# Dividing attention weights by their sums ahead of the transposition, and moving selection counts from one engine to another

## The chip, the core and the metric

The kernel runs on one core of one Trainium2 chip. The metric is the device time of one execution in microseconds (us), of the slowest core where there are several; here there is one. The engines are TensorE (PE: matmuls; PEld is its weight load), VectorE (DVE), ScalarE (ACT), GpSimd (POOL) and SyncE (SP, which issues most DMA transfers). Each runs its own list of instructions in order; they wait for each other on semaphores.

## The reference: what is computed

One inference step of a hybrid decoder of two layers, in float32, for two groups of requests that share the weights: one prompt of 512 tokens, and 8 samples of 8 tokens each with 2048 tokens of past in a paged cache. The width is 1024, with 16 query heads on 2 key/value heads (groups of 8), head dimension 64. Each layer is half an FFN (width 2688), a mixer, half an FFN. Layer 0 uses mixer A, layer 1 mixer B.

Mixer A keeps, for each query, the keys with the highest indexer scores: 128 for a prompt query, 256 of the 2056 for a sample's query. Mixer B is an attention over a window of 128 tokens with one sink per head:

```python
def sink_softmax(logits, sinks):
    m = max(max(logits, axis=-1), sinks)
    e = exp(logits - m)
    return e / (sum(e, axis=-1) + exp(sinks - m))

def sparse_attend(q, k_sel, v_sel, dist, table):     # mixer A
    logits = q @ k_sel * HEAD_DIM ** -0.5 + rel_bias(dist, table)
    return softmax(where(dist >= 0, logits, NEG)) @ v_sel

def swa_prompt(...):                                 # mixer B, blocks of 128 queries
    logits = qb @ band(k) * HEAD_DIM ** -0.5 + bias  # 256 keys, the block's and the one before
    o = sink_softmax(where(valid, logits, NEG), sinks) @ band(v)
```

## The kernel before

Activations lie feature-major in SBUF (128 features by 576 tokens: 512 of the prompt, 64 of the samples), and each weight tile is split by POOL into a high and a low part, which PE multiplies in three passes (lines 593 to 597). This takes most of the time; the change doesn't touch it.

**Prompt attention.** One function per engine, used by both mixers with `L` "A" or "B". Its work is 32 units `(r, i, g)`: four blocks `i` of 128 queries, taken in `ORDER` (0 to 3 in A, 3 to 0 in B; `r` counts the blocks as they are taken), and in each eight heads `g` per key/value head `n`. A unit is one `g` for both `n`. Block `i` in mixer A has `128 * (i + 1)` keys; in mixer B 256, and 128 in block 0. A unit goes through:
- logits on PE (strip of biases by a matmul with an identity, L745; in A for `i > 0` a mask, L740; queries by keys, L749), into the PSUM buffer `PS[u % 2]`;
- the negated row maximum on DVE (L1599), in B then a minimum with the negated sink (L1602);
- exponentials on ACT with their row sums (L1215), into `p`;
- transposition of the weights on PE (L775), copy to SBUF on ACT (`weights_of`, L1249);
- values on PE (L789), which leaves the block's unscaled outputs in PSUM.

At the end of a block the row sums are inverted (L1568; in B the sinks' exponentials `es` are added first), PE spreads the inverses over the rows (`row_scales`, L758), ACT copies them to `otok` (L1224, two halves), DVE multiplies them with the outputs (`products`, L1576, halves issued in the next block's units 1 and 2) and makes the low parts (`parts`, L1589). The high parts `XH` are made by ACT in A (L1231) and by DVE in B. The order of the instructions is written out by hand in these loops: on PE `transposed(u)`, `logits(u + 2)`, `values(u - 1)`, and `row_scales` between them in a block's last unit.

**Selection for the samples.** Beside mixer A's prompt units, the threshold of the samples' 256 best keys is found bit by bit, a step each: `decide(k)` on DVE (L1833 to L1845, small operations on one column) and then `count(k + 1)`, a pass over 1032 columns of scores. Steps up to `FOUND` = 7 come before the prompt attention; then one step follows each unit's maximum (`after(u)`, `selections`). Counts 1 to `SIGN_COUNTS` = 16 are done by ACT as sums of signs (L1375, output `maskSA`), nine of them (8 to 16) in the loop of units by

```python
def later_counts(u):
    if FOUND + 1 + u <= SIGN_COUNTS:
        count(FOUND + 1 + u)
```

the later ones by DVE itself (L1826). After the last bit, `threshold`, `sample_cut`, `sample_mask` and `block_diagonal` (the samples' queries `qbd`, spread over a zeroed tile, L1549) take a unit each.

**Samples.** `paged_sample_attention` begins on PE with `new_logits()` (L842: the samples' new keys), then transposes pages of keys (L825, `keys(b, c)`); in B, `window_sample_attention` begins with its transpositions (L912).

Of the kernel before, what the change touches and what calls it, by code (L numbers as in the profile page):

```python
# [17 lines left out]
F32 = mybir.dt.float32  # L18
# [92 lines left out]
def mixer_memory(sb, L):  # L111
# [6 lines left out]
    with ExitStack() as c:  # L118
# [79 lines left out]
        else:  # L198
# [5 lines left out]
            mb(c, "stripL", [P, KVH, GRP, 2 * P], F32R)  # L204
            with ExitStack() as c2:
                mb(c2, "stripH", [P, KVH, GRP, 2 * P], F32R)
# [4 lines left out]
            mb(c, "striproom", [P, KVH * GRP * 2 * P])  # L211
            mb(c, "vT", [P, TOK])
            with ExitStack() as c2:
                mb(c2, "strip", [P, KVH, GRP, 2 * P])
            mb(c, "p", [P, 2, KVH, SEQ])
            mb(c, "pt", [P, 2, KVH, 2, P])
            mb(c, "otok", [P, GRP, P])
# [5 lines left out]
def bass_hybrid_step(nc, io):  # L223
    at = layout()
    ctx = ExitStack()
    with ctx:
# [37 lines left out]
        with ExitStack() as c:  # L264
# [36 lines left out]
                "pt_ps", "pt_evac", "pv_ps", "ri_set", "r_ps", "r_set", "o_evac", "ot_evac", "ktS_ps", "ktS_evac", "qkS_ps", "nmS_set",  # L301
# [3 lines left out]
                      "cm_used", "seek_set", "count_set", "oh_set", "newS_ps", "newS_set", "riS_set") + tuple(f"kv_in{s}{c}" for s in range(KV_SLOTS)  # L305
                                                                   for c in range(KT_GROUPS)),
                "B": ("es_in", "es_set", "kv_in", "ptnS_evac", "esS_in", "esS_set")}
# [220 lines left out]
        def _(pool):  # L528
# [29 lines left out]

            ffn("ffn0")
            for c in range(A_CHUNKS):  # L560
                split(at["inA"][0] + c, None, 0, ND * (IDIM + IH) if c == 0 else ND * P)
            for n in range(KVH):
# [6 lines left out]
                .then_inc(MS["A"]["selb_in"], 16)  # L569
            pool.wait_ge(MS["A"]["qk_ps"], NQT * GRP)  # L570
# [14 lines left out]
        def _(pe):  # L585
# [136 lines left out]
            def prompt_attention(L, m, ms, aend):  # L722
                units = [(r, i, g) for r, i in enumerate(ORDER[L]) for g in range(GRP)]
# [4 lines left out]
                def logits(u):  # L728
                    r, i, g = units[u]
                    k0, nk = key_range(L, i)  # L730
# [4 lines left out]
                    masked, w = L == "A" and i > 0, min(nk, 2 * P)  # L735
# [7 lines left out]
                    for n in range(KVH):  # L743
                        for k, part in enumerate((m["stripH"][:, n], strip_low(L, n))):
                            mm(PS[u % 2][:, n, nk - w:nk], m["identr"][:, :], part[:, g, 2 * P - w:2 * P],  # L745
                               start=k == 0 and not masked, stop=False)
# [16 lines left out]
                turned = turned_counts(L)  # L763

                def transposed(u):

                    r, i, g = units[u]
                    nk = key_range(L, i)[1]
                    for n in range(KVH):
                        pe.wait_ge(ms["p_set"], 2 * u + n + 1)  # L770
                        out, free = turned_place(L, u, n, nk)
# [8 lines left out]
                def values(u):  # L780

                    r, i, g = units[u]
                    k0, nk = key_range(L, i)
# [3 lines left out]
                    for k in range(nk // P):  # L787
                        for n in range(KVH):
                            ins = mm(bank[6 + g // 4][n * HD:(n + 1) * HD, g % 4 * P:(g % 4 + 1) * P],  # L789
                                     m["kvtok"][:, k0 // P + k, KVW + n * HD:KVW + (n + 1) * HD],  # L790
                                     weights_of(L, u)[:, n, k, :], start=k == 0, stop=k == nk // P - 1)
# [16 lines left out]

            def paged_sample_attention(m, ms):
                LG = sample_logits  # L810
                pe.wait_ge(ms["o_evac"], 2 * NQT)
                pe.wait_ge(ms["qbd_set"], 1)
                pe.wait_ge(ms["maskS_set"], 1)
                pe.wait_ge(ms["selb_in"], 16)
# [24 lines left out]
                def new_logits():  # L839
                    for b in range(NB):  # L840
# [65 lines left out]
            def window_sample_attention(m, ms):  # L906

                pe.wait_ge(ms["o_evac"], 2 * NQT)
# [7 lines left out]
                for k, group in enumerate(LOGIT_GROUPS):  # L916
# [6 lines left out]
                    ins.then_inc(ms["qkS_ps"], 1)  # L923
                for half in range(2):
# [145 lines left out]
            prompt_attention("A", m, ms, aend)  # L1070
# [17 lines left out]
            prompt_attention("B", m, ms, aend)  # L1088
# [14 lines left out]
        def _(act):  # L1103
# [89 lines left out]
            def attention_loads(m, ms):  # L1193

                act.wait_ge(g_out, 32)
                act.dma_start(m["strip"].rearrange("p n g x -> p (n g) x"),
# [7 lines left out]
            def prompt_attention(L, m, ms, after):  # L1204
                units = [(r, i, g) for r, i in enumerate(ORDER[L]) for g in range(GRP)]
                turned = turned_counts(L)

                def exps(u):
                    r, i, g = units[u]
                    nk = key_range(L, i)[1]  # L1210
# [16 lines left out]
                def high_parts(r):  # L1227
                    i = ORDER[L][r]
# [6 lines left out]
                for u, (r, i, g) in enumerate(units):  # L1235
                    if u + 1 < len(units):
                        exps(u + 1)
                    if L == "A" and r and g == 2:
                        high_parts(r - 1)
                    if L == "B" and g == GRP - 2:  # L1240
                        act.wait_ge(ms["es_in"], r + 1)
# [851 lines left out]
```

## Time and profile before

| | |
|---|---|
| Median of 3 runs | 2341.34 us (2338.2 to 2345.47) |
| Profiled execution: time, span | 2343.02 us, 2341.2 us |
| PE busy | 2258.6 us (96%), 14801 instructions |
| PEld busy | 2029.8 us (87%) |
| DVE busy | 1137.1 us (49%) |
| POOL busy | 1029.7 us (44%) |
| ACT busy | 415.4 us (18%) |
| Chain that ended last | PE 61%, DVE 2% |

The span is the trace's time from first to last instruction, and the time is what the device reports for the same execution. Busy shares are averages over the whole span: a stage in which PE waits shows only when the trace is read by stretches. The chain is followed back from the last instruction to what released each step; its shares by line are those of the weight matmuls (lines 593 to 597, 57% together).

### The profile page before, as it was taken

How to read it: one execution, taken by the hardware profiler on the slowest of the kernel's cores; microseconds unless marked ns; L12 is line 12 of the kernel's file. 1: busy time of each engine (PE TensorE's matmuls, PEld its weight loads, DVE VectorE, ACT ScalarE, POOL GpSimd, SP SyncE). 2: the span in 40 equal slices, each digit the busy share in tenths (PEclk: the TensorE clock that was granted, in tenths of full speed). 3: DMA queues.
4: the chain of work that ended last, by engine and by line, in shares of the span. 5: the costliest groups of instructions: out<-in, count | busy, mean ns of one | idle time of the engine just before them, and what ended most of it. 6: DMA issues, size and time to landing. Idle time of an engine off the chain costs nothing.

```text
span 2341.2 us, 39794 instructions
## 1 busy us (share of the span) xinstructions
PE 2258.6 (96%) x14801; PEld 2029.8 (87%) x14819; DVE 1137.1 (49%) x1811; ACT 415.4 (18%) x848; POOL 1029.7 (44%) x622
## 2 busy tenths in 40 slices
PE   7999999999888899999999999999999999999997
PEld 6999989959666588999999999999996689999997
DVE  4544522488584546555512555542264465555311
ACT  3101000131554412010000101000015420101002
POOL 4546455414001024555555555555541055555552
PEclk9999999999799999999999999999999899999998
DMA  5435363535003433333223333322350023333221
GB/s 125 99 73 115 78 155 89 114 64 147 10 1 100 130 89 77 86 81 81 78 84 90 82 86 85 81 78 82 94 154 23 1 73 81 81 86 83 79 83 60
DMA packets 378042, 196.33 MB, mean 84 GB/s; under 512 B 66531, under 2 KB 374476, under 8 KB 377932
## 3 DMA queue, kind: packets, MB, share of 16 engines
q1 hardware_dynamic: 366108, 180.79, 31.3%
q10 hardware_dynamic: 11552, 13.71, 2.0%
q8 instruction: 62, 1.02, 0.2%
q0 software_dynamic: 288, 0.56, 0.1%
q14 instruction: 32, 0.26, 0.0%
HBM read 192.23 MB, written 11.64 MB: 87 GB/s over the span
## 4 chain that ended last, share of the span: by engine, by line
PE 61%; DVE 2%; ACTq 0%; ACT 0%; issue 0%; DVEq 0%
PE psum L594 17%; PE psum L597 11%; PE psum L595 10%; PE psum L593 10%; PE psum L596 9%; PE psum L749 1%; PE psum L775 1%; DVE XS L1448 1%; PE psum L745 1%; PE psum L789 1%; ACTq L1200 0%; PE psum L758 0%; DVE squares L1481 0%; PE psum L939 0%; PE psum L938 0%
## 5 line engine op out<-in xcount | busy, mean ns | idle before, releaser
L545 POOL CAST WSP<-WST 128x1024 fp32r<-128x1024 f32 (+1 forms) x305 | 310.5, 1018 | 1250.0 <-PE psum L597 1008.8
L547 POOL TENSOR_TENSOR WSP<-WST,WSP 128x1024 fp32r<-128x1024 f32 (+1 forms) x305 | 709.3, 2326 | 24.5
L594 PE MATMUL psum<-XS,WSP 128*128 128x512 f32 x1672 | 658.4, 394 | 0.0
L593 PE MATMUL psum<-XS,WSP 128*128 128x320 f32 x1672 | 520.4, 311 | 9.5 <-DVE XS L1448 4.3
L597 PE MATMUL psum<-XS,WSP 128*128 128x320 f32 x1672 | 522.7, 313 | 0.0
L595 PE MATMUL psum<-XS,WSP 128*128 128x320 f32 x1672 | 519.2, 311 | 0.0
L596 PE MATMUL psum<-XS,WSP 128*128 128x256 f32 x1672 | 474.0, 283 | 0.0
L596 PEld LDWEIGHTS psum<-XS,WSP 128*128 128x128 f32 x1672 | 314.8, 188 | 71.5
L593 PEld LDWEIGHTS psum<-XS,WSP 128*128 128x128 f32 x1672 | 321.4, 192 | 11.6 <-DVE XS L1448 5.2
L597 PEld LDWEIGHTS psum<-XS,WSP 128*128 128x128 f32 x1672 | 321.5, 192 | 0.0
L594 PEld LDWEIGHTS psum<-XS,WSP 128*128 128x128 f32 x1672 | 314.4, 188 | 0.4
L595 PEld LDWEIGHTS psum<-XS,WSP 128*128 128x128 f32 x1672 | 314.2, 188 | 0.0
L594 PE MATMUL psum<-GS,WSP 128*128 128x512 f32 x672 | 265.3, 395 | 0.0
L1465 DVE TENSOR_TENSOR us<-psum,rstd 128x576 f32<-128x576 f32 x84 | 63.6, 758 | 396.7 <-PE psum L597 396.5
L1488 DVE SCALAR_TENSOR_TENSOR X<-psum,X 128x576 f32<-128x576 f32 x48 | 36.4, 757 | 416.1 <-PE psum L597 416.1
L1179 ACT ACTIVATE gs<-gs 128x576 f32<-128x576 f32 x84 | 57.6, 686 | 923.1 <-DVE gs L1471 923.1
L593 PE MATMUL psum<-GS,WSP 128*128 128x320 f32 x672 | 205.9, 306 | 2.9 <-POOL WSP L547 2.9
L597 PE MATMUL psum<-GS,WSP 128*128 128x320 f32 x672 | 206.7, 308 | 0.0
L595 PE MATMUL psum<-GS,WSP 128*128 128x320 f32 x672 | 205.7, 306 | 0.0
L1528 DVE TENSOR_TENSOR us<-us,gs 128x576 f32<-128x576 f32 x84 | 187.7, 2235 | 2.9
L596 PE MATMUL psum<-GS,WSP 128*128 128x256 f32 x672 | 189.1, 281 | 0.0
L596 PEld LDWEIGHTS psum<-GS,WSP 128*128 128x128 f32 x672 | 126.3, 188 | 29.8
(325 smaller groups left out, 2595.0 us busy)
## 6 DMA issues: line engine op xcount, KB each, us to landing
WST<-in_ffn_w_gate SPq DMA_DIRECT2D x168, 256.0 KB, 3.9
WST<-in_ffn_w_up SPq DMA_DIRECT2D x168, 256.0 KB, 3.9
WST<-in_ffn_w_down SPq DMA_DIRECT2D x192, 224.0 KB, 3.5
WST<-in_a_w_in SPq DMA_DIRECT2D x28, 256.0 KB, 4.4
kv0A<-in_cache_kv SPq DMA_DIRECT2D x48, 128.0 KB, 2.3
kv2A<-in_cache_kv SPq DMA_DIRECT2D x48, 128.0 KB, 2.3
WST<-in_b_w_in SPq DMA_DIRECT2D x20, 256.0 KB, 4.0
kscr<-in_cache_idx SPq DMA_DIRECT2D x128, 32.0 KB, 2.1
```

The lines of the kernel that those rows point to most:

```text
L545: nc.gpsimd.tensor_copy(WSP[s][:, 0, 0:width], WST[s][:, 0:width]).then_inc(w_hi, 1)
L547: nc.gpsimd.tensor_tensor(WSP[s][:, 1, 0:width], WST[s][:, 0:width], WSP[s][:, 0, 0:width].bitcast(F32), ALU.subtract).then_inc(w_split, 1)
L593: mm(front, high, x[:, 0, 0:FRONT], start=first, stop=False)
L594: mm(split, high, x[:, :, FRONT:TOK], start=first, stop=False)
L595: mm(front, high, x[:, 1, 0:FRONT], start=False, stop=False)
L596: mm(back, low, x[:, 0, FRONT:TOK], start=False, stop=last)
L597: return mm(front, low, x[:, 0, 0:FRONT], start=False, stop=last)
L745: mm(PS[u % 2][:, n, nk - w:nk], m["identr"][:, :], part[:, g, 2 * P - w:2 * P], start=k == 0 and not masked, stop=False)
L1179: fn(gs[:, j % 2, :], gs[:, j % 2, :], ACT.Silu).then_inc(silu_done, 1)
L1465: steps.mark(tt(dst, acc(k)[rows], r, ALU.mult))
L1488: steps.done(stt(X[:, d, :], acc(aend + d % 2), scale, X[:, d, :], ALU.mult, ALU.add))
L1528: steps.done(tt(us[:, :], us[:, :], g, ALU.mult))
```

## The change

Two parts.

**Mixer B** gets prompt functions of its own. The sink becomes a column: the strip of biases has 258 columns instead of 256 (`SINK` = 2, the second a mask), so the maximum and the row sum of the exponentials include it, and the minimum, `es` and their waits go. Each unit's weights are multiplied by the inverse of their sums on DVE (`factors`) before PE transposes them. `row_scales`, `otok` and `products` are gone; ACT copies the outputs from PSUM to `XH`, DVE makes `XL` from PSUM and `XH`. PE's order becomes logits two units ahead, values of the unit before, transposition.

**Mixer A** keeps its functions. All counts after `FOUND` are DVE's (`later_counts` is gone), a block's last unit (`g` = 7) has no step, and the inverses of a block are computed before the next block's first maximum instead of after. `block_diagonal` is done by POOL, ahead of the output projection's weights. On PE the samples begin with the key transpositions and wait for one product only; `new_logits` follows them and takes the other waits.

The pieces of the diff below are, in this order: the build on POOL; PE's order in mixer B; PE's start of the samples in mixer A; ACT's copies in B; ACT's counts in A; the place of the inverses on DVE in A; DVE's multiplications in B; the sign of the counts; and the steps that a block's last unit skips.

```diff
+            def block_diagonal(m, ms):
+
+                pool.wait_ge(acc_evac, at["inA"][1] + A_CHUNKS + RING)
+                nc.gpsimd.memset(m["qbd"][:, :, :], 0.0).then_inc(ms["qbd_clear"], 1)
+                pool.wait_ge(ms["qbd_clear"], 1)
+                for n in range(KVH):
+                    h = slice(n * HD, (n + 1) * HD)
+                    dst = m["qbd"][h].rearrange("p b (n g t) -> p n g b t", n=KVH, g=GRP)[:, n]
+                    nc.gpsimd.tensor_copy(dst, m["qT"][h, :, SEQ:TOK].rearrange("p g (b t) -> p g b t", b=NB))\
+                        .then_inc(ms["qbd_set"], 1)
...
+                logits(0)
+                logits(1)
+                for u in range(len(units)):
+                    if u + 2 < len(units):
+                        logits(u + 2)
+                    if u:
+                        values(u - 1)
+                    transposed(u)
+                values(len(units) - 1)
...
-                new_logits()
                 keys(0, 0)
                 keys(0, 1)
                 keys(0, 2)
+                new_logits()
                 logits(0, 0)
...
+                    if g == 5:
+                        high_part(r, 0)
+                    if g == 1 and r:
+                        high_part(r - 1, 1)
...
-            def later_counts(u):
-
-                if FOUND + 1 + u <= SIGN_COUNTS:
-                    count(FOUND + 1 + u)
...
+                    if g == 0 and r:
+                        row_scales(r - 1)
                     dve.wait_ge(ms["qk_ps"], u + 1)
                     ins = nc.vector.tensor_reduce(nm, PS[u % 2][:, :, 0:nk], AX, ALU.max, negate=True)
-                    if g == 0 and r:
-                        row_scales(r - 1)
...
+                def factors(u):
+
+                    r, i, g = units[u]
+                    dve.wait_ge(ms["p_set"], 2 * (u + 1))
+                    nc.vector.reciprocal(m["ri"][:, i, :, g], m["rs"][:, i, :, g]).then_inc(ms["ri_set"], 1)
+                    dve.wait_ge(ms["ri_set"], u + 1)
+                    for n in range(KVH):
+                        p = m["p"][:, u % 2, n, 0:key_range("B", i)[1]]
+                        ts(p, p, m["ri"][:, i, n, g:g + 1], None, ALU.mult).then_inc(ms["pn_set"], 1)
...
             def sign(k):
-                return -2 ** 31 if 1 <= k <= SIGN_COUNTS else 0
+                return -2 ** 31 if 1 <= k <= FOUND else 0
...
             def selections(u):
 
-                k = found + u
+                if u % GRP == GRP - 1:
+                    return
+                k = found + u - u // GRP
```

The order of the instructions shows the change at three places. First DVE in mixer A, at units 0 and 1, where a step follows each maximum (`nmA`); before:

```order
L1599 TENSOR_REDUCE nmA<-psum 128x2 [waits qk_psA,strip_inA,dve_step]
L1833 STREAM_SHUFFLE countA<-countA 128x1 [waits count_setA]
L1840 TENSOR_SCALAR seekA<-countA 128x1 [waits dve_step]
L1841 SCALAR_TENSOR_TENSOR seekA<-seekA 128x1 [waits dve_step]
L1845 TENSOR_SCALAR seekA<-seekA 128x1 [waits seek_setA]
L1599 TENSOR_REDUCE nmA<-psum 128x2 [waits qk_psA,dve_step]
```

and now:

```order
L1706 TENSOR_REDUCE nmA<-psum 128x2 [waits qk_psA,strip_inA,dve_step]
L1968 STREAM_SHUFFLE countA<-countA 128x1 [waits count_setA]
L1975 TENSOR_SCALAR seekA<-countA 128x1 [waits dve_step]
L1976 SCALAR_TENSOR_TENSOR seekA<-seekA 128x1 [waits dve_step]
L1980 TENSOR_SCALAR seekA<-seekA 128x1 [waits seek_setA]
L1961 TENSOR_SCALAR flagsA,countA<-scsA,seekA 128x1032 [waits seek_setA,dve_step]
L1706 TENSOR_REDUCE nmA<-psum 128x2 [waits qk_psA]
```

Between two maxima the count (`flagsA,countA`) has joined the decision, and the next maximum's wait for the step is gone with it.

Second PE in mixer B, where one block of queries ends and the next begins (`ptB` are the transposed weights, `riB` the inverses of the sums); before:

```order
L775 MATMUL psum<-ident,pB 128x128 [waits pt_evacB,p_setB]
L775 MATMUL psum<-ident,pB 128x128
L758 MATMUL psum<-ident,riB 64x128 [waits ri_setB]
L758 MATMUL psum<-ident,riB 64x128 x15
L789 MATMUL psum<-ptB,kvtokB 64x128 [waits pt_evacB]
L789 MATMUL psum<-ptB,kvtokB 64x128 x3
L745 MATMUL psum<-stripHB,identrB 128x256 [waits r_setB,p_setB]
L745 MATMUL psum<-stripLB,identrB 128x256
L745 MATMUL psum<-stripHB,identrB 128x256
L745 MATMUL psum<-stripLB,identrB 128x256
L749 MATMUL psum<-kTB,qTB 128x256 x2
```

and now:

```order
L837 MATMUL psum<-stripHB,identrB 128x258 [waits p_setB]
L837 MATMUL psum<-stripLB,identrB 128x258
L837 MATMUL psum<-stripHB,identrB 128x258
L837 MATMUL psum<-stripLB,identrB 128x258
L841 MATMUL psum<-kTB,qTB 128x256 x2
L871 MATMUL psum<-ptB,kvtokB 64x128 [waits ot_evacB,pt_evacB]
L871 MATMUL psum<-ptB,kvtokB 64x128 x3
L857 MATMUL psum<-ident,pB 128x128 [waits pt_evacB,pn_setB]
L857 MATMUL psum<-ident,pB 128x128
L857 MATMUL psum<-ident,pB 128x128 [waits pt_evacB,pn_setB]
```

The sixteen small matmuls of the scales are gone, the transposition waits for the multiplied weights (`pn_setB`), and it stands behind the logits and values instead of ahead of them.

Third DVE in mixer B at the same place (`esB` are the sinks' exponents); before:

```order
L1599 TENSOR_REDUCE nmB<-psum 128x2 [waits qk_psB]
L1602 TENSOR_TENSOR nmB<-nmB,nsinkB 128x2 [waits dve_step]
L1608 TENSOR_TENSOR esB<-nmB,nsinkB 128x16 [waits nm_setB]
L1599 TENSOR_REDUCE nmB<-psum 128x2 [waits qk_psB]
L1602 TENSOR_TENSOR nmB<-nmB,nsinkB 128x2 [waits dve_step]
L1567 TENSOR_TENSOR rsB<-rsB,esB 128x16 [waits es_setB,p_setB]
L1568 RECIPROCAL riB<-rsB 128x16 [waits dve_step]
L1576 TENSOR_TENSOR otokB<-psum,otokB 128x512 [waits pv_psB,r_setB]
```

and now:

```order
L1741 TENSOR_REDUCE nmB<-psum 128x2 [waits qk_psB]
L1722 RECIPROCAL riB<-rsB 128x2 [waits p_setB]
L1726 TENSOR_SCALAR pB<-pB,riB 128x256 [waits ri_setB]
L1726 TENSOR_SCALAR pB<-pB,riB 128x256
L1733 TENSOR_TENSOR XS<-psum,XS 128x4x128 [waits oh_setB]
L1741 TENSOR_REDUCE nmB<-psum 128x2 [waits qk_psB]
```

The minimum, the additions of the sinks and the products have given way to a reciprocal of two columns and two multiplications behind each maximum.

## Rows read from the trace of the kernel before

**Rows 1.** By stretches: us, busy PE, PEld, DVE, ACT, POOL (x), PEclk, DMA share, GB/s.
```profile
595.40:624.20 28.80, 23.30 (x114) 16.36 (x114) 10.16 (x53) 18.80 (x57) 0.00 (x0) 0.58 0.01 2
688.70:726.40 37.70, 33.51 (x319) 24.09 (x318) 21.30 (x29) 21.82 (x52) 6.74 (x4) 1.00 0.15 43
1763.80:1785.20 21.40, 20.88 (x184) 14.90 (x186) 10.00 (x24) 13.69 (x46) 1.97 (x1) 1.00 0.11 26
```

**Rows 2.** Waits, 595 to 730: us in total, times, longest.
```profile
DVE countA L1833 <- ACT maskSA L1375: 21.7, 9, 2.9
```

**Rows 3.** Timeline, mixer A's first block: start us, duration us, [idle before, releaser].
```profile
598.08 0.43 DVE L1599 TENSOR_REDUCE nmA<-psum 128x2 f32<-128x256 f32 x1
...
609.27 0.42 DVE L1599 TENSOR_REDUCE nmA<-psum 128x2 f32<-128x256 f32 x1
...
610.25 0.83 PE L775 MATMUL psum<-ident,pA 128*128 128x128 f32 x2 [0.60 <-ACT pA L1215]
...
610.70 1.16 ACT L1375 ACTIVATE maskSA<-scwA,seekA 128x1032 bf16<-128x1032 f32 x1
...
611.99 0.01 DVE L1833 LOAD_MASK_SELECT countA<-countA  x1 [2.29 <-ACT maskSA L1375]
```

**Rows 4.** Timeline of DVE, mixer A's second block.
```profile
646.92 0.69 DVE L1599 TENSOR_REDUCE nmA<-psum 128x2 f32<-128x512 f32 x1
...
647.53 0.15 DVE L1833 STREAM_SHUFFLE countA<-countA 128x1 f32<-128x1 f32 x1
...
648.35 1.29 DVE L1826 TENSOR_SCALAR_CACHE_REDUCE flagsA<-scsA,seekA 128x1032 bf16<-128x1032 f32 x1
```

**Rows 5.** Timeline, mixer A's first change of blocks.
```profile
623.41 0.69 DVE L1599 TENSOR_REDUCE nmA<-psum 128x2 f32<-128x512 f32 x1
...
625.32 1.16 ACT L1375 ACTIVATE maskSA<-scwA,seekA 128x1032 bf16<-128x1032 f32 x1
...
627.83 0.60 ACT L1224 ACTIVATE otokA<-psum 128x512 f32<-128x512 f32 x1 [0.78 <-PE psum L758]
...
628.53 0.38 PE L740 MATMUL psum<-pmaskA,identb 128*128 128x256 bf16 x2 [0.53 <-issue]
...
630.05 0.69 DVE L1599 TENSOR_REDUCE nmA<-psum 128x2 f32<-128x512 f32 x1 [1.94 <-PE psum L749]
...
636.10 0.68 DVE L1599 TENSOR_REDUCE nmA<-psum 128x2 f32<-128x512 f32 x1
```

**Rows 6.** Timeline of DVE, mixer A's fourth block.
```profile
705.99 0.91 DVE L1549 MEMSET qbdA<- 128x1024 f32 x1 [0.16 <-issue]
```

**Rows 7.** Timeline of PE, start of mixer A's samples.
```profile
727.26 0.18 PE L842 MATMUL psum<-maskSA,selbA 128*128 128x8 bf16 x1 [0.86 <-DVE otokA L1576]
...
729.26 2.28 PE L825 MATMUL psum<-ident,kv0A 128*128 128x128 f32 x12
```

**Rows 8.** Timeline of PE, mixer B.
```profile
1780.32 0.66 PE L775 MATMUL psum<-ident,pB 128*128 128x128 f32 x4
...
1782.01 0.66 PE L789 MATMUL psum<-ptB,kvtokB 128*64 128x128 f32 x8
...
1782.59 0.66 PE L775 MATMUL psum<-ident,pB 128*128 128x128 f32 x4
...
1787.48 0.66 PE L775 MATMUL psum<-ident,pB 128*128 128x128 f32 x4
...
1840.09 0.68 PE L775 MATMUL psum<-ident,pB 128*128 128x128 f32 x2
...
1844.50 1.09 PE L912 MATMUL psum<-ident,kvB 128*128 128x128 f32 x8 [0.99 <-DVE otokB L1576]
```

**Rows 9.** Timeline of POOL and DVE ahead of mixer A.
```profile
586.55 4.68 POOL L566 TENSOR_TENSOR WSP<-stripA,stripHA 128x2048 fp32r<-128x2048 f32 x1 [1.67 <-PE psum L597]
...
587.25 3.99 DVE L1841 SCALAR_TENSOR_TENSOR seekA<-seekA 128x1 int32<-128x1 int32 x1
```

**Rows 10.** Groups by line and form, DVE: busy us, mean ns | idle before.
```profile
L1764 DVE TENSOR_SCALAR squares<-rPA,wisA 128x384 f32<-128x384 f32 x1 | 0.4, 420 | 1.0 <-ACT rPA L1360 1.0
```

More of the change, by code:

```diff
@@ L734, in logits @@
                         pe.wait_ge(ms["r_set"], 2 * r)
-                    masked, w = L == "A" and i > 0, min(nk, 2 * P)
+                    masked, w = i > 0, min(nk, 2 * P)
                     if masked:
@@ L807, in prompt_attention, with window_prompt_attention, logits, transposed @@
                 values(len(units) - 1)
+            def window_prompt_attention(m, ms, aend):
+                units = [(r, i, g) for r, i in enumerate(ORDER["B"]) for g in range(GRP)]
+                pe.wait_ge(acc_evac, aend + RING)
+                pe.wait_ge(ms["kvt_sb"], NTT)
+                pe.wait_ge(ms["vnew_sb"], 2)
+                def logits(u):
+                    r, i, g = units[u]
+                    k0, nk = key_range("B", i)
+                    if u > 1:
+                        pe.wait_ge(ms["p_set"], 2 * (u - 1))
+                    if u == 0:
+                        pe.wait_ge(ms["strip_set"], KVH)
+                    for n in range(KVH):
+                        for k, part in enumerate((m["stripH"][:, n], strip_low("B", n))):
+                            mm(PS[u % 2][:, n, 0:nk + SINK], m["identr"][:, :], part[:, g, 2 * P - nk:STRIP_B],
+                               start=k == 0, stop=False)
+                    for n in range(KVH):
+                        h = slice(n * HD, (n + 1) * HD)
+                        ins = mm(PS[u % 2][:, n, 0:nk], m["qT"][h, g, i * P:(i + 1) * P], m["kT"][h, k0:k0 + nk],
+                                 start=False, stop=True)
+                    ins.then_inc(ms["qk_ps"], 1)
+                turned = turned_counts("B")
+                def transposed(u):
+                    r, i, g = units[u]
+                    nk = key_range("B", i)[1]
+                    for n in range(KVH):
+                        pe.wait_ge(ms["pn_set"], 2 * u + n + 1)
+                        out, free = turned_place("B", u, n, nk)
+                        if free >= 0:
+                            pe.wait_ge(ms["pt_evac"], turned[free] if nk <= 2 * P or n else turned[free] - 1)
+                        for k in range(nk // P):
+                            ins = nc.tensor.transpose(out[:, k * P:(k + 1) * P], m["p"][:, u % 2, n, k * P:(k + 1) * P],
+                                                      ident[:, :])
+                        if n or nk > 2 * P:
+                            ins.then_inc(ms["pt_ps"], 1)
+                def values(u):
+                    r, i, g = units[u]
+                    k0, nk = key_range("B", i)
+                    pe.wait_ge(ms["pt_evac"], turned[u])
+                    if g % 4 == 0 and r > 0:
+                        pe.wait_ge(ms["ot_evac"], 2 * (r - 1) + g // 4 + 1)
+                    for k in range(nk // P):
+                        for n in range(KVH):
+                            ins = mm(bank[6 + g // 4][n * HD:(n + 1) * HD, g % 4 * P:(g % 4 + 1) * P],
+                                     m["kvtok"][:, k0 // P + k, KVW + n * HD:KVW + (n + 1) * HD],
+                                     weights_of("B", u)[:, n, k, :], start=k == 0, stop=k == nk // P - 1)
+                    ins.then_inc(ms["pv_ps"], 1)
+                logits(0)
[7 more added lines that the diff above has]
+                values(len(units) - 1)
@@ L1555, in block_diagonal, with paged_prompt_attention @@
                 ins.then_inc(ms["qbd_set"], 1)
[L1557 to L1558 removed]
+            def paged_prompt_attention(m, ms, between, after):
+                units = [(r, i, g) for r, i in enumerate(ORDER["A"]) for g in range(GRP)]
                 def row_scales(r):
[L1562 removed]
+                    i = ORDER["A"][r]
                     dve.wait_ge(ms["p_set"], 2 * GRP * (r + 1))
                     rs, ri = m["rs"][:, i], m["ri"][:, i]
[L1565 to L1567 removed]
                     nc.vector.reciprocal(ri, rs).then_inc(ms["ri_set"], 1)
```

181 lines of the change are left out of this document (112 added, 69 removed).

## The prediction

> **What bounds the kernel now.** I read the busy shares and the chain of waits first: TensorE (PE) is busy 96% of the span and nearly all of the chain is its own, so a change gains only where PE stands still or is made to do less. The two prompt stages are the places to look, and the view by stretches shows them. In mixer A's first block of queries (595.4 to 624.2 us) PE is busy 23.3 of 28.8 us at 0.58 of its clock: at about half rate. In its last block it is busy 33.5 of 37.7 us at full clock; in mixer B's first block 20.9 of 21.4 us [rows 1]. The list of waits for mixer A names the idle time: VectorE (DVE) waits 21.7 us, nine times, for ScalarE's (ACT's) sign counts [rows 2].
>
> One unit of A's first block shows the loop. DVE's maximum starts at 609.27; ACT then does exponentials, copies the weights and, from 610.70, counts (1.16 us, plus its accumulator); DVE idles 2.29 us until 611.99 and decides. The decision takes 0.82 us (below), so the next maximum starts 3.54 us after this one, and PE idles 0.60 of them [rows 3]. So at half clock PE has about 2.9 us of work, and at full clock not less than half of that, some 1.5 us. Where DVE already counts (second block), starts are 646.92 maximum, 647.53 decision, 648.35 count: 0.61 and 0.82 us. The count is recorded with 1.29 us; the maximum's 0.69 is followed 0.61 after its start, so I put 1.21. Together 2.64 us, gapless [rows 4].
>
> **Mixer A, first block.** Nine counts leave ACT for DVE. A unit becomes decision 0.82 + count 1.21 + maximum of 256 columns. The last is not priced here; 0.61 us belongs to 512 columns [rows 4], I take 0.34 by width. Sum 2.37 us on DVE, less than the chain through ACT. PE at half clock (2.9 us) would then be the bound; but then PE is never idle, and in the trace full clock returns after such a burst, so I take 2.37 us after the first units. The first unit begins late: a count stands ahead of maximum 1, which moves from 598.08 [rows 3] to about 599.3. Six more units at 2.37 bring maximum 7 to 613.5. Maximum 8 now waits for its exponentials and a reciprocal; maximum, exponentials and weights copy took 1.43 us (609.27 to 610.70), so it starts at 614.9, against 623.41 before [rows 5]: **-8.5 us**. If PE stayed at half clock, units would last 2.9: 3.2 us of it lost.
>
> **First row change.** From maximum 8 to the next logits 5.12 us pass now (623.41 to 628.53). On ACT: exponentials and weights until 625.32 (1.91 us), then the count, then two scale copies of 0.60 us, the second after a wait of 0.78 for PE's half-clocked row scales [rows 5]. Without count and wait: 1.91 + 1.2 + 0.1 = 3.2 us, **-1.9 us**.
>
> **Second block.** The ninth ACT count sits in its first unit: maximum 9 starts at 630.05, maximum 10 only at 636.10, 6.05 us [rows 5]. On DVE: maximum 0.61, step 2.03, product 0.61 = 3.25 us, -2.8. The last unit has no step (0.82 + 1.21), but the next maximum now stands behind exponentials and reciprocal (about 1.3): together **-3.5 us**.
>
> **Third and fourth blocks.** PE's own work sets these units (33.5 of 37.7 us at full clock in the fourth [rows 1]), so a DVE step more or less moves nothing by itself. What happens: the 27 steps skip each last unit, so the threshold pass falls in unit 27 instead of 24, cut in 28, mask in 29. Unit 27 also has the low parts, and behind them now the threshold before maximum 28: decision 0.82, two passes of 1.21 and some small steps, 3.6 us. In exchange the block-diagonal build (memset 0.91 us and two copies, 1.8 us with them) leaves DVE; today it delays that same maximum [rows 6]. So maximum 28 comes 1.8 us later after maximum 27, but 27 itself is 1 to 2 us earlier, since mask and cut no longer precede it. I take **0**, from -1 to +3: PE may idle some 2 us there, and at half clock afterwards it would pay about two more.
>
> **Start of the samples.** PE waits 0.86 us for the last product, does eight small pairs (727.26 to 729.26), then three transposed key groups [rows 7]. The key groups now come first, after one product only, while the second is made. Gain: the 0.86 us wait, and some of what comes behind it because ACT's key copies start beside the pairs; I take **-1.4 us** (-0.8 to -2.0). Page loads start from the same event (all prompt logits done), so they move along.
>
> **The build on GpSimd (POOL).** Memset and two copies stand after the strips and before the out-projection's weights, right after the last queries at about 595; POOL has nothing else there (0.00 us busy in the first block [rows 1]), so POOL itself pays nothing. DVE may. At 587.25 a one-column DVE operation with two SBUF inputs took 3.99 us, ending as POOL's 4.68 us subtraction ended [rows 9]. One such decision meets the copies: between 0 and 2 us, I take **+0.5**. The Trainium skill, "SBUF — State Buffer", section "Who interferes with whom", says that a VectorE instruction with two SBUF inputs fully blocks against a GpSimd instruction that reads SBUF, and one that only writes is harmless; by that rule the memset is free and each copy can hold the decision once, and the trace's 3.99 us agrees. The same rule speaks against the new multiplications in B, since scaling one SBUF tensor may take both ports; by it each would wait out a POOL subtraction.
>
> **Mixer B.** Removed: minimum with the sinks per unit, a sink exponential and the row scales per block (PE, then two ACT copies), copies to otok, products, and XH made on DVE. Added per unit on DVE: a reciprocal of two columns and two multiplications of 256 columns. The trace has one of 384 columns from SBUF at 0.420 us [rows 10]; I take 0.35 each, so with the small steps at 0.2 some 0.8 us, bounded by 0.6 and 1.0. ACT gets two high parts per block for the two scale copies that it loses. The matmuls of 258 columns instead of 256 cost nothing I can price.
>
> Does the new chain stay hidden? PE's order is now logits u+2, values u-1, transposition u. The rhythm is 2.27 us (1780.32 to 1782.59), all PE's work, values 0.58 of it (1782.01) [rows 8]; I split the rest into 1.27 for logits and 0.42 for the transposition. The exponentials of u end no later than logits u+2 begin, then 1.27 and 0.58 us run before the transposition needs the 0.8 us of scaling: 1.0 us of slack. DVE per unit: 0.61 + 0.8, plus 0.61 per half block, under 2.27. POOL works only in the stage's first 2 us (1.97 busy, one instruction [rows 1]), before the first scaling. In the last block a unit has half the columns and hardly any slack; I give back 0.7 us.
>
> What goes: a row change puts 4.89 us between transpositions (1782.59 to 1787.48) instead of 2.27 [rows 8]: 2.6 us and 0.3 of after-effects, three times: -8.7. At the end, 4.41 us lie between the last transposition and the samples' first (1840.09 to 1844.50) [rows 8]; the new transposition waits 1.0 us longer for its scaling, but then only weights copy and values follow (about 1.2 us): -2.2. The start gains 0.4 (no minimum, logits 2 ahead). Sum -8.7 - 2.2 - 0.4 + 0.7 = **-10.6 us**.
>
> **Sum.** A: -8.5 - 1.9 - 3.5 + 0 - 1.4 + 0.5 = -14.8. With B: -25.4 us. The profiled execution has a span of 2341.2 us and a time of 2343.0, hence 2317.6 by its own time; that execution is 1.7 us above the median of 2341.3. I state 2316.5, between the two bases.
>
> **Rivals.**
> 1. *PE stays at half clock in A's first block.* For: it runs at 0.58 now [rows 1], and at 2.37 us a unit it would still be idle a third of the time once fast. Against: at half rate it would have no idle time at all. Price 3.2 us, the wait for row scales 0.8, and with a cold stretch in the fourth block 2: 2323.
> 2. *The multiplications are exposed in B.* If exponential, reciprocal, multiplication, transposition and copy do not fit ahead of PE's need, every transposition waits. It decides from a chain 1.0 us longer than my 0.8, for instance through a pass twice as slow plus waits. At 0.8 us beyond the slack, 32 units cost 26 us: about 2342, no gain; at 1 us beyond it, 2349, slower. Against it: DVE has only 10.0 us of work in 21.4 there [rows 1].
> 3. *Half of A's gain vanishes since DVE's steps, moved later, stall the fourth block*: each of six steps exposed by 1 us: 2322.
> 4. *More is hidden than I see* (PE quickly warm, little late work): 2311.
>
> **How the numbers follow.** Differences under 0.3%, 7 us, can hardly be told from no change. Chances: forecast with its neighbours, 2311 to 2321, 0.64; rivals 1 and 3, 0.22; rival 4, 0.08; rival 2 0.06, two thirds of it within 0.3% or slower. Eight in ten lie in 2309 to 2325. Faster 0.95, same 0.03, slower 0.02.
>
> **What would show it.** In A's first block, maxima every 2.4 us with counts between them, no wait of DVE for ACT, and the clock well above 0.58; the third and fourth blocks as long as now within 2 us; no DVE operation over 2 us at 597 us. In B: transpositions every 2.27 us straight through the row changes, some 10 us less from its first logits to the samples, PE never waiting for the multiplications except in the last block. Wrong would be: PE waiting for pB's scaling in most units, or A's first block still above 25 us.

## The result and the profile after

The changed kernel took 2324.34 us (median of 7 runs, 2318.01 to 2332.19), the kernel before 2345.0 (7 runs); the ratio, of the means, is 0.9922, 95% interval 0.9898 to 0.9946: 0.8% faster, 18 us, with 12.7 to 23.9 in the interval. The forecast was 25. A second set of 6 runs, beside 10 of the kernel before, gave 0.9936 (0.9921 to 0.9951), 15 us.

The page of the profiled execution (2326.41 us):

```profile
span 2324.6 us, 39568 instructions
PE 2253.7 (97%) x14691; PEld 2022.9 (87%) x14691; DVE 1156.4 (50%) x1863; ACT 405.1 (17%) x826; POOL 1033.0 (44%) x625
PE 62%; DVE 2%; ACT 0%; issue 0%; DVEq 0%; ACTq 0%
```

Against the profile before, PE's own work is 5 us less and PE stands still 12 us less. The view by stretches, for mixer A's first and fourth block and mixer B's first units (columns as in [rows 1]):

```profile
594.30:616.80 22.50, 22.17 (x110) 16.55 (x111) 17.04 (x62) 11.24 (x42) 2.16 (x3) 0.51 0.01 3
682.00:720.80 38.80, 35.38 (x316) 25.11 (x315) 25.30 (x48) 20.99 (x50) 7.70 (x5) 0.96 0.15 44
1754.80:1776.20 21.40, 20.61 (x167) 14.41 (x168) 14.90 (x39) 13.23 (x44) 1.99 (x1) 1.00 0.10 25
```

The first row is the surprise. PE is busy 22.17 of 22.50 us, at a granted clock of 0.51: the 21.7 us of waits for the counts [rows 2] are gone, and PE, at its lower level (1.2 GHz), has become the bound. DVE's maxima show it:

```profile
605.40 0.42 DVE L1706 TENSOR_REDUCE nmA<-psum 128x2 f32<-128x256 f32 x1
...
607.77 0.42 DVE L1706 TENSOR_REDUCE nmA<-psum 128x2 f32<-128x256 f32 x1
...
610.46 0.43 DVE L1706 TENSOR_REDUCE nmA<-psum 128x2 f32<-128x256 f32 x1 [0.22 <-PE psum L762]
...
613.18 0.43 DVE L1706 TENSOR_REDUCE nmA<-psum 128x2 f32<-128x256 f32 x1 [0.26 <-PE psum L762]
...
616.86 0.69 DVE L1706 TENSOR_REDUCE nmA<-psum 128x2 f32<-128x512 f32 x1 [2.12 <-PE psum L762]
...
623.94 0.69 DVE L1706 TENSOR_REDUCE nmA<-psum 128x2 f32<-128x512 f32 x1 [2.61 <-PE psum L762]
```

They are 2.37 us apart up to 607.77, then 2.7, waiting for PE's logits (L762), against 3.54 before. PE is the slower one already before that: its transpositions are 2.72 us apart, and DVE's 2.37 only use up the units by which PE's logits are ahead. The last step, from 613.18 to 616.86, takes 3.68 us, of which DVE waits 2.12: here PE makes the wider logits of the second block (256 keys), still at half clock.

```profile
605.53 0.69 PE L788 MATMUL psum<-ident,pA 128*128 128x128 f32 x2
608.25 0.69 PE L788 MATMUL psum<-ident,pA 128*128 128x128 f32 x2
...
613.69 0.69 PE L788 MATMUL psum<-ident,pA 128*128 128x128 f32 x2
617.37 0.69 PE L788 MATMUL psum<-ident,pA 128*128 128x128 f32 x2
```

From 616.86 to 623.94, the first change of blocks, 7.08 us pass, no less than the 6.64 before [rows 5], although ACT's count is gone. PE makes its row scales at half clock in both, in 3.68 us here and 3.47 before; in all other traces of the changed mixer A they take 1.97.

```profile
617.99 3.68 PE L771 MATMUL psum<-ident,riA 128*64 128x128 f32 x32
...
623.82 0.65 PE L788 MATMUL psum<-ident,pA 128*128 128x128 f32 x4
```

In the kernel before:

```profile
624.31 3.47 PE L758 MATMUL psum<-ident,riA 128*64 128x128 f32 x32 [2.79 <-DVE riA L1568]
```

In mixer B the transpositions run on through the changes of blocks, and PE waits only at the end:

```profile
1773.46 0.66 PE L857 MATMUL psum<-ident,pB 128*128 128x128 f32 x4
...
1775.88 0.66 PE L857 MATMUL psum<-ident,pB 128*128 128x128 f32 x4
...
1778.17 0.66 PE L857 MATMUL psum<-ident,pB 128*128 128x128 f32 x4
...
1823.88 0.44 PE L871 MATMUL psum<-ptB,kvtokB 128*64 128x128 f32 x4 [0.53 <-ACT ptB L1370]
...
1825.34 0.44 PE L871 MATMUL psum<-ptB,kvtokB 128*64 128x128 f32 x4 [0.66 <-ACT ptB L1370]
...
1826.68 0.48 PE L871 MATMUL psum<-ptB,kvtokB 128*64 128x128 f32 x4 [0.53 <-ACT ptB L1370]
...
1827.09 1.97 PE L989 MATMUL psum<-ident,kvB 128*128 128x128 f32 x8
```

1775.88 to 1778.17 is a change of blocks: 2.29 us, where 4.89 stood [rows 8].

**Where the time came from**, by the two profiles, in us counted from each stage's first logits. "Other runs" are the traces of five of the runs below in which mixer A's prompt units are coded as in the changed kernel (A alone, multiplications twice, old order in B, old start, and the changed kernel again).

| Stretch | Forecast | This trace | Other runs |
|---|---|---|---|
| A, to maximum 8 (28.04 before) | -8.5 | -5.5 | -5.5 to -6.0 |
| A, maximum 8 to 9 (6.64) | -1.9 | +0.4 | -1.7 to -1.8 |
| A, maximum 9 to 16 (24.80) | -3.5 | -2.0 | -1.8 to -3.5 |
| A, maximum 16 to 24 (30.54) | 0 | -0.1 | -0.1 to -0.2 |
| A, maximum 24 to last transposition (36.25) | 0 | +1.6 | +0.4 to +2.7 |
| A, from there to the output projection (120.25) | -1.4 | -2.0 | -1.3 to -3.8 |
| **A, all** | -14.8 (port +0.5) | -7.5 | -8.8 to -12.7 |
| **B**, first logits to output projection (102.65) | -10.6 | -7.8 | -7.7 to -7.8 (B alone, old start, changed kernel again) |

Of the six this execution gained least in A; their mean is -10.2. With B's -7.8 that makes -18, as timed. The two profiled executions themselves differ by 16.6 us in span: 15.3 in these two stages, the rest elsewhere.

### The profile page after: what moved, and what is told of

The parts are those of the page before. It is cut to its first block, busy times and chain, and to the rows that moved or that the text cites. A ratio compares the mean times of both kernels' runs of the same rounds, so it can differ in the third digit from the quotient of the medians.

```text
span 2324.6 us, 39568 instructions
## 1 busy us (share of the span) xinstructions
PE 2253.7 (97%) x14691; PEld 2022.9 (87%) x14691; DVE 1156.4 (50%) x1863; ACT 405.1 (17%) x826; POOL 1033.0 (44%) x625
## 4 chain that ended last, share of the span: by engine, by line
PE 62%; DVE 2%; ACT 0%; issue 0%; DVEq 0%; ACTq 0%
PE psum L607 17%; PE psum L610 11%; PE psum L608 11%; PE psum L606 11%; PE psum L609 9%; DVE XS L1560 1%; PE psum L841 1%; PE psum L871 1%; PE psum L857 1%; PE psum L837 1%; DVE squares L1593 0%; PE psum L1016 0%; PE psum L1017 0%; PE psum L627 0%; PE psum L692 0%
## 5 line engine op out<-in xcount | busy, mean ns | idle before, releaser
L606 PEld LDWEIGHTS psum<-XS,WSP 128*128 128x128 f32 x1672 | 321.4, 192 | 12.7 <-DVE XS L1560 5.2
```

What stands on the lines that cost most here:

```text
L606: mm(front, high, x[:, 0, 0:FRONT], start=first, stop=False)
```

## The experiments

**The parts alone.** The kernel before with all of A's edits, and the changed kernel with A's edits undone; of each the core.

```diff
-            prompt_attention("A", m, ms, later_counts)
+            prompt_attention("A", m, ms, lambda u: None)
...
-                k = found + u
+                if u % GRP == GRP - 1:
+                    return
+                k = found + u - u // GRP
```

```diff
+                    if FOUND + 1 + u <= SIGN_COUNTS:
+                        count(FOUND + 1 + u)
...
-BITS, FOUND = 32, 7
+BITS, SIGN_COUNTS, FOUND = 32, 16, 7
```

> Mixer A's part alone, mixer B as before. If the two parts are independent, as the stage lengths of the profile after say (mixer A's stage 7.5 us shorter, B's 7.3), this is 7.5 us (0.3%) faster than the kernel before: ratio 0.9968, and mixer A's stage in the trace is as long as in the changed kernel to within 1 us. Rival: the late steps or the clock carry over from one part to the other; then the gain is under 4 us or over 11.

> Mixer B's part alone, mixer A as before. Independent parts: 7.3 us faster, ratio 0.9969, from PE's first logits of B to the samples' products as in the changed kernel. My prediction had 10.6 us for this part (0.9955); if the prediction was right and only the one profile of the changed kernel came out short, this shows it.

Measured: A alone 0.9954 (0.9937 to 0.9971), 10.8 us; B alone 0.9969 (0.9957 to 0.9980), 7.3 us. They add up. B is as the trace said: 102.65 us became 94.99. For A my expectation was 7.5 us, from the one profile. The time doesn't exclude it (6.8 to 14.8 in the interval), but the trace missed it: it gained 12.7 us (233.79 against 246.52 us to the output projection), with the code that had 238.99 in the changed kernel's trace. The two differ in how long PE had half clock. In the changed kernel it lasts from 595 to 622 us; in A alone it had ended before that point, which shows as 0.86:

```profile
600.00:612.00 12.00, 12.00 (x66) 8.77 (x63) 10.50 (x35) 4.93 (x23) 0.00 (x0) 0.50 0.01 1
612.00:618.00 6.00, 5.48 (x57) 4.23 (x56) 3.44 (x10) 3.24 (x12) 0.00 (x0) 0.86 0.00 0
```

So the row scales ran at full clock, and the change of blocks took 4.85 us instead of 7.08.

**Does idle time bring the half clock?** PE stands still for 2.63 us ahead of mixer A, and then again for its first exponentials. Fillers (transpositions of an identity into an unused part of PSUM) close the first gap, and in the second kernel also load units 1 to 7.

```diff
+                def fill(k):
+                    for _ in range(k):
+                        nc.tensor.transpose(bank[7][:, 3 * P:4 * P], ident[:, :], ident[:, :])
+
+                fill(24)
                 pe.wait_ge(acc_evac, aend + RING)
...
+                    if 0 < u < GRP:
+                        fill(5)
                     transposed(u)
```

> The changed kernel with 24 transpositions of an identity by PE, into an unused part of PSUM, in the 2.6 us in which it waits for the last queries ahead of mixer A. They fill idle time and compute nothing that is used. Theory 1 (that idle time is what drops the clock to half for the whole first block): the granted clock stays at 1.00, units of the first block go by DVE at 2.37 us instead of 2.72, the row scales take 2.0 instead of 3.7 us, the stage is some 4 us shorter. Theory 2 (the load of the first block's units sets the clock, whatever comes ahead of them): half clock begins a few us later than 594.7 us or at the same place, the stage is less than 1 us shorter.

> As the run before, and 5 such transpositions ahead of each transposition in units 1 to 7 of mixer A's first block as well: 0.5 us of PE work at full clock, 1.05 at half. If PE's load keeps the clock up (theory 2 in its strong form), the clock is 1.00 through the first block, units last 2.37 us and the stage is some 4 us shorter than in the changed kernel. If the clock drops whatever PE does, units last 2.72 + 1.05 = 3.8 us and the stage is 7 us longer.

With the first gap filled, the clock held through the first logits and fell behind PE's wait of 1.48 us for its first exponentials:

```profile
599.68 0.68 PE L794 MATMUL psum<-ident,pA 128*128 128x128 f32 x2 [1.48 <-ACT pA L1299]
```

The stretches: filler, first logits with that wait, rest of the block:

```profile
593.30:596.10 2.80, 2.80 (x26) 2.57 (x24) 2.60 (x11) 1.25 (x2) 0.00 (x0) 1.00 0.88 165
596.10:600.40 4.30, 2.80 (x22) 2.16 (x21) 3.35 (x15) 3.36 (x8) 2.16 (x3) 1.00 0.05 9
600.40:616.00 15.60, 15.60 (x84) 11.92 (x83) 13.63 (x48) 7.65 (x35) 0.00 (x0) 0.52 0.00 1
```

The gap ahead of the stage is thus not what holds the clock down for the whole block; theory 1 is out as I put it. Maximum 8 came at 21.77 us, 0.8 us earlier than in the changed kernel. With the units loaded as well:

```profile
593.40:597.00 3.60, 2.12 (x18) 1.65 (x17) 2.64 (x11) 3.05 (x6) 2.16 (x3) 1.00 0.07 14
597.00:601.90 4.90, 4.88 (x29) 4.08 (x29) 4.62 (x17) 2.46 (x12) 0.00 (x0) 0.65 0.00 0
601.90:613.00 11.10, 11.10 (x101) 8.90 (x98) 9.66 (x37) 5.40 (x25) 0.00 (x0) 1.00 0.01 1
```

The clock still fell after the same wait (0.65), but was back by 601.9. Units are 2.37 us, and maximum 8 comes after 19.54 us: 8.5 less than before. That is the forecast's number, and by its steps: 3.8 us to maximum 1 (forecast 3.9), 18.1 to maximum 7 (18.1), 1.47 for the last step (1.4). The times were 0.9923 (0.9905 to 0.9941) and 0.9921 (0.9902 to 0.9940): neither can be told from the changed kernel's, so the fillers are shown in the trace only.

**The counts alone.** The nine counts back on ACT.

```diff
+                    if g < GRP - 1 and FOUND + 1 + u - u // GRP <= SIGN_COUNTS:
+                        count(FOUND + 1 + u - u // GRP)
```

> The changed kernel with the nine counts of units 0 to 9 done by ACT again (none in a block's last unit); all else as changed. If the counts' move is the gain in mixer A's first block, its units are 3.53 us again and the stage is about 8 us longer than in the changed kernel, at a first block at half clock in both. If PE at half clock were the bound in either case, the loss would be only the difference of 3.53 and 2.72: 6 us over seven units, with the first change of blocks unchanged.

Measured 0.9961 (0.9947 to 0.9975), 9 us of the 18 lost. Maximum 8 came at 25.97 us against 22.57, and maxima 9 to 16 took 26.2 us against 22.8: 3.4 and 3.5. The units of the first block were 3.53 us again, as expected, but from maximum 7 to 8 only 1.47 us passed instead of 3.68, since PE wasn't behind. The first change of blocks took 5.0 us, with the count gone from it. So both of my cases were too high for the first block (8 and 6), and the second block, which I had left out of them, carries as much. It holds two counts on ACT here, where the kernel before had one, so this run doesn't give the price of the change's own move in that block. The stage took 243.11 us, 4 to 9 more than in the six traces.

**The late steps.** A step in every unit, the last of a block too.

```diff
-                if u % GRP == GRP - 1:
-                    return
-                k = found + u - u // GRP
+                k = found + u
```

> The changed kernel with a step of the selection in every unit again, the last of a block too, so that threshold, cut and mask fall in units 24 to 26 instead of 27 to 29. If the late steps are what lengthens the fourth block of mixer A (last transposition 1.6 us later than before, in the profile after, counted from the block's start), the fourth block gets shorter by about 1.5 us, and each change of blocks longer by up to 2.0 us (a decision and a count ahead of the inverses, 0.82 + 1.21), if it isn't hidden by PE's row scales. Rival: the fourth block's loss comes from the half clock that PE had for 3.4 us there; then the length of the block follows the clock and not the steps.

Measured 0.9912 (0.9885 to 0.9939). Fourth block, maximum 24 to last transposition: 34.76 us, against 36.67 to 38.91 in the six traces of the table; of these, the one without any half clock in the block has the 36.67. So the late steps cost 1.9 us, and the half clock around their stall up to 2.2 more. Change of blocks: 4.86 us, nothing lost by the step in the last unit. What the skip does in the changed kernel, DVE around maxima 27 and 28:

```profile
691.50 1.22 DVE L1706 TENSOR_REDUCE nmA<-psum 128x2 f32<-128x1024 f32 x1
694.75 1.29 DVE L1694 TENSOR_TENSOR XS<-otokA,XS 128x512 fp32r<-128x512 f32 x2 [2.03 <-ACT XS L1309]
...
697.17 1.29 DVE L2054 TENSOR_SCALAR_CACHE_REDUCE flagsA<-scsA,cutA 128x1032 bf16<-128x1032 f32 x1
...
698.39 1.28 DVE L2055 TENSOR_SCALAR_CACHE_REDUCE scwA<-scsA,cutA 128x1032 f32<-128x1032 f32 x1
...
699.60 1.22 DVE L1706 TENSOR_REDUCE nmA<-psum 128x2 f32<-128x1024 f32 x1
```

and on PE, behind them:

```profile
702.93 1.12 PE L788 MATMUL psum<-ident,pA 128*128 128x128 f32 x8 [2.95 <-ACT pt_odd L1324]
```

Two low parts (1.29, after 2.03 of waiting for ACT's high parts) and the threshold (2.6 and small steps) meet between two maxima, 8.10 us apart, and PE stands still for 2.95. Without the skip the longest wait of PE in this block is 1.33 us.

**Mixer B: how much slack?** The multiplications twice (the first pair into a scratch tile), and PE's old order.

```diff
+                    for n in range(KVH):
+                        p = m["p"][:, u % 2, n, 0:key_range("B", i)[1]]
+                        ts(squares[:, n, 0:key_range("B", i)[1]], p, m["ri"][:, i, n, g:g + 1], None, ALU.mult)
...
                 for u in range(len(units)):
+                    transposed(u)
                     if u + 2 < len(units):
                         logits(u + 2)
                     if u:
                         values(u - 1)
-                    transposed(u)
```

> The changed kernel with the two multiplications of each unit of mixer B done twice (the first pair into a scratch tile, nothing reads it): 0.62 us more on DVE in every unit. If the multiplications have slack (in the trace after they end 1.34 us ahead of the transposition), units keep 2.29 us, and B's stage (first logits to first output projection, 94.9 us after) grows by under 3 us, all of it where DVE also has a low part or in the short last block. If they are on the path, every unit grows by 0.6 us, 20 us in all.

> The changed kernel with PE's order in mixer B as it was before: transposition, logits two ahead, values. If the new order is what hides the multiplications, PE now waits at each transposition for exponentials, reciprocal and multiplications of the same unit: at least 0.5 us a unit, B's stage over 12 us longer. If the chain would be hidden in the old order too, the stage is within 2 us of the 94.9 of after.

Twice: one execution of 2324.0 us, transpositions still 2.29 us apart, the samples reached after 74.02 us instead of 72.27 and the output projection after 99.68 instead of 94.89; 3 us of that come after the samples' start, at half clock, and aren't the multiplications': the kernel with loaded units, whose mixer B is the changed kernel's, had 98.21 the same way. Old order: one execution of 2350.41 us, slower than each of 13 of the kernel before (at most 2347.58); the stage took 116.97 us, 22 more. Its waits and units:

```profile
PE psum L857 <- DVE pB L1726: 20.7, 31, 1.3
```

```profile
1774.31 0.70 PE L857 MATMUL psum<-ident,pB 128*128 128x128 f32 x4 [0.67 <-DVE pB L1726]
...
1777.38 0.70 PE L857 MATMUL psum<-ident,pB 128*128 128x128 f32 x4 [0.67 <-DVE pB L1726]
```

Dividing ahead of the transposition is a gain only with the new order; with the old one PE waits 0.67 us in each unit.

**The start of the samples** as before the change, with its waits ahead too.

```diff
+                new_logits()
                 keys(0, 0)
                 keys(0, 1)
                 keys(0, 2)
-                new_logits()
```

> The changed kernel with PE's start of the samples in mixer A as before: all waits ahead, the new keys first, then the three groups of transposed keys. If the new order gives what the stage lengths say, the stretch from the last transposition of the prompt units to the output projection is 120.2 us as before the change, instead of 116.4 to 118.9 in the four traces with the new order; if the gain there is the chance of the clock, it stays inside 116.4 to 118.9.

One execution, 2319.75 us. From the last transposition to the samples' first instruction 5.62 us pass, as before, instead of 4.69; to the output projection 118.14, no longer than with the new order. The 0.9 us are won at the start and don't reach the end of the stage.

**A better version.** The changed kernel again, and two built on the kernel without the skip. In them the low parts of a block stand apart, where ACT's high parts are ready; the last also has the fillers, 14 of them ahead of the first transposition.

```diff
-                    if g == 3 and r:
-                        parts(r - 1)
+                    if g in (4, 5) and r:
+                        parts(r - 1, (g - 4,))
                     after(u)
```

> The changed kernel itself, on the chip of the three that follow, to compare them with, and a second trace of it. Executions with this same code for mixer A (four traces so far) differ: its first block had PE at half clock for 20.5 or 27.3 us, and from its first logits to the output projection 233.8 to 239.0 us. The time should be 0.992 to 0.993 of the kernel before's; if the first trace was typical, mixer A's stage is 239 us again; if it was the exception, nearer to 234.5.

> A step of the selection in every unit (as the run without the skip), and the low parts of the block before, which stand together in a block's fourth unit and wait there for ACT's high parts (1.61 us, and two subtractions), now one in the fifth and one in the sixth unit. If the late steps and this wait are both on the path, mixer A's stage is another 5 to 7 us shorter than without the skip (230.7 us): unit four of each block loses its 2 to 3 us. If they aren't, it is as there, and the time stays 0.991 of before.

> As the run before, with transpositions of an identity on PE in the idle time ahead of mixer A (24), ahead of the first transposition (14) and in units 1 to 7 (5 each). If idle time of PE brings the half clock, PE keeps full clock through the first block and the stage is 2 to 4 us shorter than in the run before (units 2.37 instead of 2.72 us, row scales 2.0 instead of 3.7). If the clock falls for another reason, the fill costs 1.05 us a unit at half clock and the stage is up to 7 us longer.

Measured: changed kernel 0.9936 (0.9921 to 0.9951); parts apart 0.9890 (0.9873 to 0.9908), 2314.86 us; with fillers 0.9890 (0.9872 to 0.9908), 2314.2. Parts apart is faster than the kernel before and the changed kernel; against the version without the skip (0.9885 to 0.9939) the times don't decide. To the output projection its mixer A takes 228.09 us (238.99 and 236.29 in the two traces of the changed kernel, the second between the 239 and 234.5 that I had named; 230.74 without the skip): 2.7 less than without the skip, where I had expected 5 to 7. The wait is gone, but each part takes its 0.61 us elsewhere. In the second block, DVE:

```profile
627.97 0.69 DVE L1706 TENSOR_REDUCE nmA<-psum 128x2 f32<-128x512 f32 x1
...
630.61 0.69 DVE L1706 TENSOR_REDUCE nmA<-psum 128x2 f32<-128x512 f32 x1
631.21 0.68 DVE L1694 TENSOR_TENSOR XS<-otokA,XS 128x512 fp32r<-128x512 f32 x1
...
633.85 0.69 DVE L1706 TENSOR_REDUCE nmA<-psum 128x2 f32<-128x512 f32 x1
```

With the fillers the clock stays at 1.00 through the first block, and the stage is 1.3 us shorter again (226.79), under what the times can show:

```profile
593.10:616.10 23.00, 22.11 (x200) 17.54 (x199) 20.92 (x77) 12.58 (x49) 2.16 (x3) 1.00 0.01 2
```

## Why the prediction was wrong: the mechanisms held, the sizes didn't

The mechanisms held, but the sum was 7 us too large: 25 us forecast, 18 measured (ratio 0.9894 forecast, 0.9922 measured), and 2324.34 us lies outside the forecast's neighbourhood of 2311 to 2321. The step that failed first is "full clock returns after such a burst, so I take 2.37 us": PE stayed at half clock, and the -8.5 us of A's first block measured -5.5. By its own steps:

- **First block, -8.5.** The unit on DVE was right (2.37 us), and so is the 8.5 at full clock (the run with loaded units). Wrong was "in the trace full clock returns after such a burst". PE was busy 22.17 of 22.50 us at 0.51 of its clock. The trace before had a row against it, in this very block:

```profile
600.00:605.00 5.00, 5.00 (x27) 3.98 (x26) 1.18 (x8) 3.57 (x10) 0.00 (x0) 0.50 0.00 0
```

  This is rival 1, which I gave too little. Half clock costs 2.5 to 3.0 us in the six traces, against the 3.2 of its price, but that the sizes meet is in part luck. I had all of it in six units of 2.9 us. PE's unit is 2.72, its logits made ahead hid most of the difference (0.8 us were lost by maximum 7), and 1.7 to 2.3 us came in the step to maximum 8 (3.2 to 3.7 us instead of 1.4), for which neither the sum nor the rival had PE's wider logits at half clock.
- **First row change, -1.9.** -1.7 to -1.8 in five of six traces, in all of which the row scales ran at full clock (1.97 us), unlike before. In the profiled execution they took 3.68 us: +0.4. So the missing count alone gained nothing there; the gain needs the clock.
- **Second block, -3.5.** Right in two of six traces. PE waits 2.7 us in the block's fourth unit, behind DVE's low parts, in all six; in four of them it falls to half clock there, and 1.5 us are lost. Why not in the other two isn't shown.
- **Fourth block, 0 (-1 to +3).** +1.6 here. The picture was right: maximum 27 comes 1.5 us earlier, 28 follows it 1.55 us later than before. I took 0 because the two cancel; but PE's wait behind maximum 28, which I put at "some 2 us", was 2.95, and with the half clock after it came on top. The skip of the last units, which causes it, saves nothing elsewhere.
- **Port, +0.5.** Nothing: no two-input operation of DVE fell into POOL's copies (595.31 to 596.58); the nearest, at 594.59 (beside POOL's memset) and 596.68, took 0.16 us each. The Trainium skill's rule ("SBUF — State Buffer", section "Who interferes with whom") had no case to apply to.
- **Samples, -1.4.** 0.9 at their start as worked out. That the stage was 2 us shorter in the end isn't explained by it, since the old start had that too. What makes this is open. The granted clock of the stretch was 0.94 in both traces of the old mixer A and 0.96 to 0.97 in the six new ones; no run separates the two.
- **Mixer B, -10.6.** The chain was hidden, with 1.34 us of slack where I had 1.0. The changes of blocks gave 2.60, 2.61 and 2.34 us, as the 2.6 said, but the 0.3 of after-effects for each didn't exist: -7.6 for my -8.7. The end gave 3.0 instead of 2.2 (4.41 became 1.38). Where I had a gain of 0.4 at the start stands the price of the new order: the first transposition comes 4.54 us behind the first logits instead of 2.97, 1.6 us, and units 1 to 7 took 0.7 more. That makes -8.4 at the samples, and a stretch of half clock right there (1827.09: 1.97 us for what took 1.09) gives 0.7 back.

Most of the shortfall is thus two terms: some 5 us in A for the clock and the late steps, 3 us in B for the start and the after-effects. Rival 1's total of 2323 us has the measured ratio (0.9922), which is luck too: it has B at -10.6.

Between 600 and 616 us PE was busy 16.00 of 16.00 us in the changed kernel, at 0.50 of its clock, the lower level. The Trainium skill, "TensorE: Matmul & The Clock Gate", section "What's actually happening", says that PE gets full clock after a sustained busy stretch. By the profile's busy share, the trace disagrees for this block.

## What to carry to other kernels

When a wait is removed from a stage where PE runs at half clock, the next bound can be PE at that clock: work out PE's own time per unit at both levels, also for the wider unit that follows the stage, and take the slower one unless a row shows the clock rising in that very stage. Where work is moved later to spare one point, look at what it meets at its new place. And one profile is one draw: six traces of the same code in mixer A differed by 5 us, more than most terms of the sum.

## What the runs showed of the hardware

- The time of an execution goes with its mean granted clock. The changed kernel took 2318 us at 0.985 and 0.987, 2324 to 2326 us at 0.982, and 2330 to 2332 us at 0.981 and 0.979.
- In mixer A's first block PE stayed at half clock for some 20 us in five traces and 27 us in one, although from its first transposition on it was busy all the time; ahead of that it had waited 0.3 to 1.5 us. With five small transpositions more per unit it was back at full clock within the next units, after the same wait; I can say what it did ahead of the rise, not why that was enough.
- In two kernels with fillers the clock fell behind a wait of 1.48 us at the start of mixer A; when that wait was filled too (beside the low parts set apart), it stayed at 1.00.
